# First attention's probabilities turned in 32x32 pieces by VectorE and moved inside SBUF, read by TensorE one round later

## What is computed

```python
z = h @ w_in[l]
u, gb, gc, q, k, v = jnp.split(z, splits, axis=-1)
y_conv = gb * short_conv(gc * u, conv_w[l])
q = rms_norm(q.reshape(B, S, N_HEADS, HEAD_DIM), g_q[l]) * (HEAD_DIM ** -0.5)
k = rms_norm(k.reshape(B, S, N_HEADS, HEAD_DIM), g_k[l])
y_attn = dilated_mixture(q, k, v).reshape(B, S, D_ATTN)
mix = jnp.concatenate([rms_norm(y_conv, g_conv_out[l]), rms_norm(y_attn, g_attn_out[l])], axis=-1)
x = x + mix @ w_out[l]
```

## Time and profile before

| | us |
|---|---|
| three runs | 1002.47, 1003.67, 1003.82 |
| median | 1003.67 |
| the profiled execution, its own time | 1004.4 |
| its span, first to last instruction | 1001.6 |
| TensorE busy | 983.9 (98%) |
| VectorE busy | 684.2 (68%) |
| ScalarE busy | 439.1 (44%) |
| DMA queue 1 (SP), share of 16 engines | 29.1% |
| DMA queue 0 (POOL), share of 16 engines | 6.0% |

### The profile page before, as it was taken

The page is one execution under the profiler, slowest core; times in us unless marked ns, Lnnn a source line. Parts: engine busy times, 40 slices in busy tenths (PEclk is TensorE's granted clock), DMA queues, the critical chain, the costliest instruction groups (busy, mean ns, idle before and its releaser), DMA issues. The chain is left out here.

```text
span 1001.6 us, 14462 instructions
## 1 busy us (share of the span) xinstructions
PE 983.9 (98%) x4732; PEld 798.4 (80%) x4732; DVE 684.2 (68%) x1221; ACT 439.1 (44%) x729; POOL 157.7 (16%) x274
## 2 busy tenths in 40 slices
PE   6999999999999999999999999999999999999997
PEld 6887787777888888888888877888888887677886
DVE  7787786797667667555426668498978764665656
ACT  5656666644323233233221236945542325563343
POOL 3000100200000000964000001835750000000000
PEclk9999999999999999999999999999999999999999
DMA  7244624352533323244223223322233332123332
GB/s 229 85 144 130 204 76 139 77 155 73 178 100 90 105 85 104 88 143 149 88 102 102 86 75 109 102 85 65 63 105 96 92 105 63 43 64 86 106 93 84
DMA packets 144305, 104.31 MB, mean 104 GB/s; under 512 B 4717, under 2 KB 136045, under 8 KB 144269
## 3 DMA queue, kind: packets, MB, share of 16 engines
q1 hardware_dynamic: 138768, 85.83, 29.1%
q0 software_dynamic: 5264, 17.97, 6.0%
q10 hardware_dynamic: 236, 0.06, 0.0%
HBM read 99.65 MB, written 4.20 MB: 104 GB/s over the span
## 5 line engine op out<-in xcount | busy, mean ns | idle before, releaser
L591 PE MATMUL bank<-hH,wH 128*128 128x512 f32 x840 | 328.7, 391 | 0.1
L593 PE MATMUL bank<-hH,wL 128*128 128x512 f32 x840 | 327.0, 389 | 0.0
L592 PE MATMUL bank<-hL,wH 128*128 128x512 f32 x840 | 326.9, 389 | 0.0
L1506 DVE TENSOR_TENSOR wL<-raw,wH 128x1024 fp32r<-128x1024 f32 x155 | 196.1, 1266 | 129.2 <-ACT wH L1074 128.2
L1074 ACT ACTIVATE wH<-raw 128x1024 fp32r<-128x1024 f32 x155 | 164.2, 1059 | 264.4 <-PE bank L593 136.1
L591 PEld LDWEIGHTS bank<-hH,wH 128*128 128x128 f32 x840 | 157.7, 188 | 36.9 <-issue 2.9
L593 PEld LDWEIGHTS bank<-hH,wL 128*128 128x128 f32 x840 | 157.7, 188 | 32.9
L592 PEld LDWEIGHTS bank<-hL,wH 128*128 128x128 f32 x840 | 157.8, 188 | 32.1
L835 PE MATMUL bank<-aH,wH 128*128 (+1 forms) x160 | 62.2, 389 | 0.0
L836 PE MATMUL bank<-aL,wH 128*128 (+1 forms) x160 | 62.2, 389 | 0.0
L837 PE MATMUL bank<-aH,wL 128*128 (+1 forms) x160 | 62.2, 389 | 0.0
(11 more groups left out here) (478 smaller groups left out, 1548.5 us busy)
## 6 DMA issues: line engine op xcount, KB each, us to landing
raw<-in_w_in_dram SPq DMA_DIRECT2D x61, 512.0 KB, 3.6
mraw<-in_w_mod_dram POOLq DMA_DIRECT2D x24, 512.0 KB, 4.6
raw<-in_w_gate_dram SPq DMA_DIRECT2D x22, 512.0 KB, 3.7
raw<-in_w_up_dram SPq DMA_DIRECT2D x22, 512.0 KB, 3.7
raw<-in_w_down_dram SPq DMA_DIRECT2D x22, 512.0 KB, 3.3
raw<-in_w_out_dram SPq DMA_DIRECT2D x16, 512.0 KB, 3.5
x_tok<-in_x_dram SPq DMA_DIRECT2D x4, 512.0 KB, 5.6
rotations<-eb POOLq DMA_DIRECT2D x4, 512.0 KB, 5.0
```

The lines of the kernel that those rows point to most:

```text
L591: mm(o, a, hH[:, k, :], start=(k == 0), stop=False)
L592: mm(o, a, hL[:, k, :], start=False, stop=False)
L593: ins = mm(o, b, hH[:, k, :], start=False, stop=(k == KD - 1))
L1506: TT(wL[s.par][:], raw[s.par][:], wH[s.par][:].bitcast(F32), SU).then_inc(lo_done, 1)
```

## The change

The first attention's rounds 0, 1 and 2 no longer transpose on TensorE. VectorE turns each 128-query block of probabilities in 32x32 pieces (`turn`, a `transpose` instruction) into `turned`; POOL's queue moves `turned` with four DMAs to `pTd` (`turned_moves`), where 32 of 128 partitions go to all 128, four rows of pieces behind each other; TensorE reads `pTd` in runs of 32 columns in the next round, between projections gc and gb (`weigh(..., pieces=True)`). Since partition 4p+j of a moved block holds key 32j+p, ScalarE writes `vT` with the keys in that order. The last round keeps `attend` with TensorE's transposes, so it puts v's keys back in their own order, with 16 matmuls against the identity in place of four transposes.

The scores of the first attention take the plain form, two heads side by side. The maximum is written negated by VectorE's own instruction, so the step that negated it goes, in both attentions, and each exponential waits for its own block's maximum and not for a head's or for all eight. `mod_rows` are put elsewhere. In `attend`, for both attentions, the first of the weighing matmuls waits for the last of the eight copies; before, each key block waited for its own.

```diff
-            def mod_loads(i):
+            def turned_moves(a):
+
+                pool.wait_ge(turn_rdy, 2 * TB * (a + 1))
+                pool.wait_ge(o_free, a + 1)
+                settled(pool)
+                for q in range(TB):
+                    pool.dma_start(pTd[:, q].rearrange("p b c -> p (b c)"),
+                                   turned[32 * q:32 * q + 32].rearrange("p j b c -> p j (b c)")).then_inc(turn_in, 16)
+                pool.wait_ge(turn_in, 16 * TB * (a + 1))
+                settled(pool)
+
+            def mod_loads(i, between=None):
                 for m in range(6):
+                    if m == 2 and between is not None:
+                        between()
                     pool.wait_ge(m_used, i * 6 + (m + 2))
...
-            def attend(a, v, vcol):
+            def weigh(a, v, vcol, pieces=False):
+
+                wait(pe, o_free, a + 1)
+                for kb in range(TB):
+                    for hh in range(2):
+                        r = slice(HD * hh, HD * hh + HD)
+                        p = (pTd[:, :, place_of(hh, kb), :].rearrange("p i b c -> p b i c") if pieces
+                             else pT[:, hh, OFF[kb]:OFF[kb + 1]])
...
+            def attend(a, n, v, vcol):
...
-                wait(pe, o_free, a + 1)
-                for kb in range(TB):
-                    pe.wait_ge(t_free, a * 8 + (kb + 9))
...
+                pe.wait_ge(t_free, n * 8 + 12)
+                weigh(a, v, vcol)
...
-            def mix(i, last):
-                for j in range(3):
-                    project(Slot(3, j, 6, i))
+            def mix(i, first, last):
+                project(Slot(3, 0, 6, i))
+                project(Slot(3, 1, 6, i))
+                if not first:
+                    pe.wait_ge(turn_in, 16 * TB * i)
+                    weigh(i - 1, vtok, pair_cols, True)
+                project(Slot(3, 2, 6, i))
                 freed(pe, Slot(2, 0, 6, i))
-                transposes(PB[3], [vT[:, blkc(b)] for b in range(TB)]).then_inc(vtr, 1)
+                if last:
+                    for b in range(TB):
+                        for j in range(TB):
+                            ins = mm(PB[3][32 * j:32 * j + 32, blkc(b)], vT[:, P * b + j:P * b + P:TB], ident,
+                                     start=True, stop=True, skip_group_check=True)
+                    ins.then_inc(vtr, 1)
+                else:
+                    transposes(PB[3], [vT[:, blkc(b)] for b in range(TB)]).then_inc(vtr, 1)
                 pe.wait_ge(ss_rd, i * 2 + 2)
                 pe.wait_ge(xt_done, KD)
-                pe.wait_ge(q_lo, i + 1)
-                split_scores(i)
+                pe.wait_ge(qn_rdy, i * 2 + 2)
+                scores(i, qn, kn)
...
+            def turn(hh, qb):
+
+                v.transpose(turned[:, :, places(hh, qb), :].rearrange("p j b c -> p b j c"),
+                            L[:, hh, CB[qb]:CB[qb + 1]].rearrange("p (b j c) -> p b j c", j=TB, c=32)
+                            ).then_inc(turn_rdy, 1)
...
+                    if turning is not None:
+                        if hh:
+                            turning()
+                        dve.wait_ge(pn, a * 2 + (hh + 1))
+                        for b in range(TB):
+                            turn(hh, b)
...
-                    score_max(i, masks1)
+                    head_max(i, masks1)
                     split_lo(gb.next())
+                if not first:
+                    mod_rows(i - 1, range(4, 6))
                 dve.wait_ge(ych, i + 2)
...
-                if not last:
-                    mod_rows(i, range(0, 2))
-                normalise(i)
+                normalise(i, None if last else lambda: split_lo(Slot(3, 3, 6, i).next()))
...
-                    split_lo(Slot(3, 3, 6, i).next())
-                    mod_rows(i, range(2, 4))
+                    mod_rows(i, range(0, 2))
                     split_lo(Slot(3, 4, 6, i).next())
-                    mod_rows(i, range(4, 6))
                     split_lo(Slot(3, 5, 6, i).next())
```

More of the change, by code:

```diff
@@ L1156, in head_rsqrt, with softmax @@
                     A(r[:], r[:], ACT.Exp, scale=-0.5).then_inc(rs_rdy, 1)
[L1158 to L1168, removed]
+            def softmax(a, order):
+                for u, (hh, b) in enumerate(order):
+                    act.wait_ge(sc_free, a * 8 + (u + 1 + 4))
+                    c = 4 * hh + b
+                    l = L[:, hh, CB[b]:CB[b + 1]]
+                    ins = A(l, l, ACT.Exp, bias=nmx[:, c:c + 1], scale=-1.0, accum_out=rs[:, c:c + 1])
+                    if b == TB - 1:
+                        ins.then_inc(ex, 1)
@@ L1192, in mix @@
                 split_hi(u.next())
-                key_high(1)
                 used(gc)
                 split_hi(gc.next())
+                if not first:
+                    values_out(i - 1)
                 used(gb)
@@ L1210, in mix @@
                     split_hi(Slot(6, 2, 6, i).next())
[L1211 to L1214 removed]
+                if last:
+                    values_out(i)
             def dyn(t, k):
@@ L1685, in mod_rows, with values_low, mix @@
                     STT(o, mraw[m % 2][:], col(csil, i * 2 + m // 3), o, MU, AD).then_inc(m_used, 1)
-            def mix(i, last):
+            def values_low(a):
+                dve.wait_ge(o_free, a + 2)
+                mark(TT(ssa[:], ssa[:], sqa[:], AD))
+                mark(STT(dyn(mixL, a + KH), yo[:], col(vec, a + V_GATT), dyn(mixH, a + KH).bitcast(F32), MU, SU))
+            def mix(i, first, last):
                 qk_norm(i)
                 u, gc, gb = (Slot(3, j, 6, i) for j in range(3))
-                def key_low(e):
-                    r = slice(HD * e, HD * e + HD)
-                    TT(k1L[e][0:HD, :], kn[r, :], k1[e][r, :].bitcast(F32), SU)
-                    return TT(k1L[e][HD:P, :], kn[r, :], k1[e][r, :].bitcast(F32), SU)
-                dve.wait_ge(q_hi, i * 2 + 1)
-                TT(q1[0][HD:P, :], qn[0:HD, :], q1[0][0:HD, :].bitcast(F32), SU)
-                TT(q1[1][0:HD, :], qn[HD:P, :], q1[1][HD:P, :].bitcast(F32), SU)
-                key_low(0)
                 split_lo(u.next())
-                dve.wait_ge(q_hi, i * 2 + 2)
-                key_low(1).then_inc(q_lo, 1)
+                if not first:
+                    mod_rows(i - 1, range(2, 4))
                 used(gc)
@@ L1711, in mix @@
                 mark(STT(cv[:], cuP[:, 0:S], col(vec, i + V_CONV), cv[:], MU, AD))
+                if not first:
+                    values_low(i - 1)
                 used(gb)
```

123 lines of the change are left out of this document (58 added, 65 removed).

## The result

| | before | after |
|---|---|---|
| median of 20 runs each | 1003.62 (1002.47 to 1004.53) | 1005.59 (1003.99 to 1007.18) |
| ratio, 95% interval | | 1.0023 [1.0016, 1.0029] |
| profiled execution, its own time | 1004.4 | 1005.98 |
| its span | 1001.6 | 1004.1 |

What follows compares the result with a forecast made beforehand. TensorE, busy 98% of the span, was taken as the bound. The terms -8.2 + 0.2 + 0.3 + 0.6 + 4.1 + 2.4 + 2.0 - 0.7 gave +0.7 us, a median of 1004.3 (no change); range 1000.0 to 1008.8.

Steps and rivals of the forecast that it cites:

- changes of form: First attention: plain scores cost +0.2 us over four rounds, and the moved weighing with a projection behind it +0.3.
- projection v: Rounds 1 and 2: VectorE delivers the split for projection v late, TensorE stands 1.2 us each time, +2.4 us.
- thg: Second attention: exponentials run ahead of the last maxima, so `thg` no longer holds TensorE; -0.7 us with the change of form.
- eighth copy: Weighing in `attend` waits for the eighth copy instead of the fifth, 0.82 us in each of five places, +4.1 us.
- Removed: Rounds 0, 1 and 2: 20 transposes each leave TensorE, with ScalarE's copies they waited for, 2.74 us each, -8.2 us.
- rival 5: The change takes no work from the path, since TensorE waits in the rounds anyway: 1012.5 us, chance 0.01.
- The last round's v: Last round: 16 fp32 matmuls of 32 columns (0.98 us) replace four transposes (0.36), +0.6 us.
- cv_split: Round 3: two `macc` steps ahead of VectorE's last convolution step make cv_split late for TensorE, +2.0 us.
- Moves: Four moves of 320 KB land in about 7 us, against a limit of about 11, so nothing waits: 0.
- Rival 4: Moves run one behind the other, 18.4 us, so scores of rounds 1 to 3 wait: 1019 us, chance 0.06.
- Rivals 2 and 3: 2: turns at twice the price, 1008.1 us, chance 0.19. 3: pieces read at half the rate, 1011.2 us, chance 0.07.
- Rival 1: The stalls at projection v and cv_split don't come, 4.4 us fall away: 999.9 us, chance 0.25.

Runs made afterwards that it cites:

- the three edits together: Changed kernel with each key block waiting for its own copy, last round's macc steps behind the divisions, `ssc` and `mixL` behind the turns: 996.74 us, 0.9938 of before.
- the run with slim moves: Changed kernel, but in rounds 1 and 2 each move takes one row of pieces of twenty, so weighing reads stale pieces: 1004.33 us, ratio 1.0011 to before.
- the two with `values_low` late: Changed kernel with `values_low` behind projection u's split in rounds 1 and 2, alone (1005.79 us) and together with three other edits (997.65 us).
- the run with the loads freed: Changed kernel, but POOL's third and fourth loads don't wait for the moves, and their macc steps precede projection gb's split: 1005.67 us, ratio 1.0026 to before.
- the runs with `ssc` late: Changed kernel with `ssc` and `mixL` behind the second head's turns in rounds 0 to 2: alone 1002.53 us, with two other edits 996.74, with three 997.65.
- the macc steps moved: Changed kernel, but in rounds 1 and 2 two macc steps stand behind the second head's turns, the other two one split later: 1006.43 us, ratio 1.0031 to before.

## Why the prediction came out as it did

The sum said +0.7 us and +2.0 were measured: right in sign, 1.3 short, and inside the forecast's 2 us by 0.1. Part of that closeness is luck: the errors of the terms have both signs (waits for the maxima +1.65, changes of form +1.1, projection v -0.5, `thg` -0.3, eighth copy -0.2). Term by term, from the two profiled executions, in which +2.54 stand at the last weighing:

- **Removed, -8.2.** Right. Round 0, where nothing waits, is shorter by the transposes and the weighing that left it but for 0.33 us (below), and the three edits together end 6.3 us below the kernel before; rival 5, that the work was not on the path, is out.
- **The last round's v, +0.6.** 178.21 to 179.25, 1.04 for 0.36: +0.7. The group of the same shape priced it.
- **Eighth copy, 5 x 0.82.** 3.51 us for 2.79 between the first transpose and the weighing, +0.73 in the last round; 0.74 in the second attention's first round, and 0.80 in each that follows (19.70 from weighing to weighing, for 18.90): 3.9 in the trace, 3.7 by the run that undoes it.
- **Projection v, 2 x 1.2.** VectorE was as forecast in round 1: turns of a head 1.61 (1.6), the split ready at T + 15.4 (15.2). TensorE came at T + 14.8 and not 14.2, since changes of form and 0.24 of waiting held it; in round 2 the late maxima shift both by the same. So 0.67 of idle time each. The projections q, k and v with their start take 17.52 us for 16.57 in round 0, 0.95 more, +1.9 in all; what the 0.28 beside the idle time is no run shows.
- **cv_split, +2.0.** From the first group of `mixH` to the one behind it 6.07 us for 4.11: +2.0.
- **thg, -0.7.** The last round of the second attention is 18.26 for 18.48, with the 0.8 of the eighth copy in it: -1.0.
- **Form changes, +0.5.** Too small. Also the sums behind a projection, v's four transposes (54.48 to 55.01, 0.53 for 0.36) and every neighbour of the moved weighing pay some 0.1 to 0.2. Round 0, in which nothing waits, is 37.52 us for 42.24 - 2.74 - 2.31 = 37.19: +0.33. What is left over in rounds 1 to 3 when the waits and v are taken out is 0.51, 0.52 and 0.28: about +1.6 in all.
- **Moves, 0.** This is the step that failed. I took "about 7" us for the moves by loads of other queues that run beside each other, and set the limit at 11. They took 11.6, 13.55 and 12.75, and round 2's scores wait 1.41: +1.4 us in this execution (1.2 by the medians of the run with slim moves). The limit was nearly right: the wait begins at about 12.1 by the estimate above. Rival 4 had the mechanism and the place where it decides, 11.7 us; it got a chance of 0.06 and a price for 18.4 us. The Trainium skill (SBUF — State Buffer, "Can I just issue two DMAs to hit both halves?") says that transfers issued together hardly gain, and by its figures the prediction had an estimate of 8.9 us; the trace agrees with the direction and lies 2.7 to 4.7 above the number, with weight loads running beside. That estimate was nearer than my row.
- **Round 1's scores, 0.** 0.24 us that the sum did not have, and not from the moves: VectorE was idle 2.43 us ahead of that gb product, and the wait is 0.23 to 0.25 in every run but the two with `values_low` late, which have none, whether round 0's moves landed after 10.8 or 12.4 us. Why the place of `values_low` matters there stays open.

These terms make -8.2 + 0.7 + 3.9 + 1.9 + 2.0 - 1.0 + 1.6 + 1.4 + 0.24 = +2.5. The two executions also differ by +0.38 at the start and -0.37 between the attentions, which no run here explains; at the start the runs of one same order differ by up to 0.9 (36.47 to 37.41).

By its own list of signs the prediction was wrong on this point: a wait on `mraw` (0.69, at 129.90) stands ahead of the late maxima. Two more signs went the same way. A middle round was to be 1.5 us shorter; round 1 is 1.0 shorter (41.19 for 42.23, between the norm's sums) and round 2 is 0.1 longer. And the moves were to land well ahead of the weighing, some 9 us by the forecast's numbers; in round 1 it was 2.1 (125.80, 127.86).

What I had not considered is that the moves have a second victim. I asked only when TensorE wants `pTd`, and when POOL's third load comes; the weight for projection gb, on SP's queue, lies in the same 15 us and came 3.7 us after ScalarE was ready for it. In the changed kernel this second lateness is hidden: with its split done VectorE still stood 0.69 us for `mraw`, so the 1.41 us came by the chain that the prediction had named (moves, third load, step, product). But it is the next limit, as the run with the loads freed shows. The run with slim moves shows that the bytes matter, and in the runs with `ssc` late the moves, issued 1.3 us earlier against TensorE, took 1.3 to 3.1 us less in round 1. Why they did is not shown: an earlier start alone is not the rule, since with the macc steps moved they were issued 0.6 later against TensorE and took 10.96.

Rivals 2 and 3 are out: turns cost 1.61 a head, pieces are read in 2.30 us. Rival 1 did not come: the waits that it had away, for projection v and for cv_split, all stand in the trace.

## What to carry to other kernels

A bulk move inside SBUF is to be priced against every load that is in flight in its time, each with its own user, not only against the reader of what is moved. When work leaves TensorE for an engine with idle time, list what that engine's next deliveries are and which has the least cover: here 1.3 us of sums and differences that nobody needed for a round stood ahead of a weight that TensorE was waiting for. A wait merged for convenience (four into one) is free only when something else can run meanwhile; in an in-order engine it cost 0.73 to 0.87 us each time, five times in the changed kernel, and more than the change lost.

## What the runs showed of the hardware

- TensorE reads fp32 probabilities in runs of 32 columns, 128 bytes, as fast as contiguous ones: 16 matmul records take 2.30 us in both.
- VectorE's transposes in 32x32 pieces, written with a stride, take 1.61 us for 1280 columns in four instructions, 1.26 ns a column, close to the 1.21 of the single ones.
- Four moves of 320 KB from 32 to 128 partitions took 10.7 to 13.8 us from issue to all landed, over all runs that move them whole with the loads behind; single ones in the changed kernel 4.5, 7.0 and 11.2 (least, median, most). In the stretch from 112 to 127 us the view of DMA lists their 1.31 MB with 49.3% of the sixteen engines' time, and 1.39 MB on SP's queue with 30.9%; two weight loads of that stretch landed 10.6 us behind their issue, where the profile's page has 3.5 over all 61:

```profile
q0 software_dynamic: 320, 1.31, 49.3%
q1 hardware_dynamic: 2758, 1.39, 30.9%
...
raw<-in_w_in_dram SPq DMA_DIRECT2D x2, 512.0 KB, 10.6
```

In this stretch a byte of the moves held the DMA engines 1.7 times as long as a byte of a load from memory.
